# Border sums of residual times output: GpSimd products added by VectorE, or diagonals of TensorE products

## The reference, cut to what matters

```python
h = x
for layer in range(DEPTH):
    ...
    u = rms_norm_2(h, norm_g[layer, 0]) * (1.0 + sc1) + sh1
    ...
    y = mixer(u, ...)                       # ends with ... @ w_out
    h = h + (1.0 + g1) * rms_norm_2(y, norm_g[layer, 1])
    u = rms_norm_2(h, norm_g[layer, 2]) * (1.0 + sc2) + sh2
    y = swiglu_ffn(u, ffn_w_in[layer], ffn_w_out[layer])
    h = h + (1.0 + g2) * rms_norm_2(y, norm_g[layer, 3])
```

## Time and profile before

| | |
|---|---|
| median of 3 runs | 3499.42 us (3499.22 to 3500.74) |
| profiled execution | 3502.82 us, of it span 3501.0 us |
| mean granted TensorE clock | 0.973 |
| busy: PE, DVE, ACT, POOL | 95%, 57%, 37%, 2% of the span |
| POOL | 57.5 us in 59 instructions |

### The profile page before, as it was taken

How to read it: one execution, slowest core, us unless ns; L and a number is a source line. 1 busy time by engine, 2 the same in 40 slices (tenths; PEclk the granted TensorE clock), 3 DMA queues, 4 the chain that set the end, 5 groups by cost and what they waited for, 6 DMA issues and landing times.

```text
span 3501.0 us, 42504 instructions
## 1 busy us (share of the span) xinstructions
PE 3308.8 (95%) x17578; PEld 2729.0 (78%) x17578; DVE 2005.5 (57%) x2799; ACT 1312.5 (37%) x1947; POOL 57.5 (2%) x59
## 2 busy tenths in 40 slices
PE   7898988999999998999989999999899999889998
PEld 3685567888888755888887888888788888788887
DVE  6777665777556476565556656333654554563334
ACT  3323544231333245533355445222523332362223
POOL 0000000000000000000000010000100000010000
PEclk8999999999999999999999999999999999999999
DMA  4541022444444230265532222222143233223321
GB/s 175 178 139 43 13 79 67 157 151 155 148 157 138 82 88 3 95 209 186 174 90 69 73 73 85 97 96 88 53 103 86 68 91 78 64 75 106 97 94 52
DMA packets 374831, 356.11 MB, mean 102 GB/s; under 512 B 73407, under 2 KB 320494, under 8 KB 373231
## 3 DMA queue, kind: packets, MB, share of 16 engines
q1 hardware_dynamic: 374419, 353.32, 33.0%
q10 hardware_dynamic: 220, 0.07, 0.0%
HBM read 345.50 MB, written 4.72 MB: 100 GB/s over the span
## 4 chain that ended last, share of the span: by engine, by line
PE 49%; DVE 5%; ACT 4%; issue 1%; POOL 0%; DMA 0%; SPq 0%; ACTq 0%; DVEq 0%; POOLq 0%
PE ps L403 44%; PE ps L2715 1%; DVE r_st L2598 1%; PE ps L2736 1%; DVE second_w_lo L570 1%; ACT second_w_hi L511 1%; PE ps L2725 1%; ACT second_scr L712 1%; DVE sums L487 1%; DVE x_res L896 0%; PE ps L2738 0%; DVE second_scr L894 0%; POOL sq L470 0%; DMA ring<-in_ffn_w_in 0%; PE ps L2444 0%
## 5 line engine op out<-in xcount | busy, mean ns | idle before, releaser
L403 PE MATMUL ps<-second_h_hi,second_w_hi 128*128 128x512 f32 (+1 forms) x2216 | 823.9, 372 | 43.7 <-DVE second_h_lo L922 17.6
L403 PE MATMUL ps<-second_h_hi,second_w_lo 128*128 128x512 f32 (+1 forms) x2216 | 809.7, 365 | 0.0
L403 PE MATMUL ps<-second_h_lo,second_w_hi 128*128 128x512 f32 (+1 forms) x2216 | 809.4, 365 | 0.0
L570 DVE TENSOR_TENSOR second_w_lo<-ring,second_w_hi 128x2048 fp32r<-128x2048 f32 (+2 forms) x176 | 373.7, 2124 | 458.5 <-ACT second_w_hi L511 458.5
L403 PEld LDWEIGHTS ps<-second_h_hi,second_w_hi 128*128 128x128 f32 x2216 | 428.4, 193 | 109.7 <-issue 28.0
L403 PEld LDWEIGHTS ps<-second_h_hi,second_w_lo 128*128 128x128 f32 x2216 | 427.7, 193 | 65.7
L403 PEld LDWEIGHTS ps<-second_h_lo,second_w_hi 128*128 128x128 f32 x2216 | 428.5, 193 | 61.5
L511 ACT ACTIVATE second_w_hi<-ring 128x2048 fp32r<-128x2048 f32 (+2 forms) x176 | 311.9, 1772 | 289.3 <-PE ps L403 280.6
L403 PE MATMUL ps<-h_mix_hi,w_hi 128*128 128x512 f32 (+3 forms) x776 | 273.4, 352 | 20.5 <-DVE h_mix_lo L739 12.6
L403 PE MATMUL ps<-h_mix_lo,w_hi 128*128 128x512 f32 (+3 forms) x776 | 270.1, 348 | 0.0
L403 PE MATMUL ps<-h_mix_hi,w_lo 128*128 128x512 f32 (+3 forms) x776 | 269.3, 347 | 0.0
(11 more groups left out here) (451 smaller groups left out, 5402.1 us busy)
## 6 DMA issues: line engine op xcount, KB each, us to landing
ring<-in_w_mlp SPq DMA_DIRECT2D x64, 1024.0 KB, 5.3
side_w<-in_ada_w SPq DMA_DIRECT2D x96, 512.0 KB, 4.8
ring<-in_ffn_w_in SPq DMA_DIRECT2D x44, 1024.0 KB, 5.1
side_w<-in_w_mod SPq DMA_DIRECT2D x80, 512.0 KB, 3.8
ring<-in_attn_w_in SPq DMA_DIRECT2D x48, 512.0 KB, 5.2
ring<-in_hgrn_w_in SPq DMA_DIRECT2D x32, 512.0 KB, 4.9
ring<-in_ffn_w_out SPq DMA_DIRECT2D x16, 1024.0 KB, 4.9
ring<-in_w_in SPq DMA_DIRECT2D x14, 1024.0 KB, 5.5
```

Source lines behind the costliest of these rows:

```text
L403: mm = pe.matmul(acc, lhsT, rhs, start=k == 0 and wp == ap, stop=k == j.kt - 1 and wp == 1)
L570: dve.tensor_tensor(unit.place(unit.slot[1]), unit.place(M.ring[:, u % RING, :]), unit.place(unit.slot[0]), ALU.subtract).then_inc(*S.w_lo ...
```

## The change

POOL's products, and the middle part of DVE's adds, are gone. In their place PE multiplies, for each tile and half, x (128 features x 128 tokens, transposed) by g·y (128 x 128), in float32, and accumulates over the eight tiles in PSUM bank 6: the diagonal of each 128x128 result is the cross sum of these tokens, spread over partitions. DVE multiplies the two accumulated results of a half by the identity (`keep_cross`, one instruction of 128x256 out of PSUM), and PE's product with ones sums it (L845). A cross block stands in PE's list 0.8 of a job behind its tile and waits for ACT's g·y. The product with ones for Σ(g·y)² (L843) now follows half a position behind that for Σy² (L837) and waits for ACT's reading of the bank. DVE adds two parts instead of three and waits for ACT alone.

Two other tables change with it. FFN_PARTS is 3, 4, 4 units, so that a late job has 8 k steps, 24 products. LeaveThread starts half 0 4.5 positions behind its border, takes the first four feature tiles of both token groups first, so that it needs one residual batch to start, has ACT copy three blocks of four, and writes 512 features per DMA.

```diff
     def add_half(self, dve, j):
         S, acc = self.S, j.sums[3]
-        parts = slice(0, 1 if j.sums_last else 3)
...
+        parts = slice(0, 1) if j.sums_last else slice(0, 3, 2)
+        dve.wait_ge(S["sums_act"].sem, S["sums_act"].at(j.sum_nth + 1))
...
-    def add_sums(self, pool, j):
-        S = self.S
-        y, x, _, acc, fresh = j.sums
-        for sig, n in j.sums_after:
-            pool.wait_ge(sig.sem, sig.at(n))
-        pool.wait_ge(S["sums_act"].sem, S["sums_act"].at(j.sum_nth + 1))
-        if fresh:
-            pool.tensor_tensor(acc[:, 1, :], y, x, ALU.mult).then_inc(*S["sums_added"].one)
-            return
-        if not j.sums_last:
-            pool.tensor_tensor(self.scratch(j)[:, 1, :], y, x, ALU.mult).then_inc(*S["sums_product"].one)
...
         pe.matmul(M.ps[:, self.SUM_BANK, 0:b - a], M.ones[:, :], M.sums[:, 0, a:b], start=True, stop=True)\
             .then_inc(*S["norm_sum"].one)
         if self.last:
             return
-        for i in (1, 2):
-            mm = pe.matmul(M.ps[:, self.SECOND_BANK, (i - 1) * (b - a):i * (b - a)], M.ones[:, :], M.sums[:, i, a:b],
-                           start=True, stop=True)
-        mm.then_inc(*S["post_sum"].one)
+        yield self.start + 1.75
+        pe.wait_ge(S["norm_ln"].sem, S["norm_ln"].at(self.first + 1))
+        pe.matmul(M.ps[:, self.SUM_BANK, b - a:2 * (b - a)], M.ones[:, :], M.sums[:, 2, a:b], start=True, stop=True)
+        pe.wait_ge(S["cross_kept"].sem, S["cross_kept"].at(n + 1))
+        pe.matmul(M.ps[:, self.SUM_BANK, 0:b - a], M.ones[:, :], M.sums[:, 1, a:b], start=True, stop=True)\
+            .then_inc(*S["post_sum"].one)
+
+    def cross_products(self, pe):
+        S, M, n, a, b = self.S, self.M, self.post, self.a, self.b
+        for i, j in enumerate(self.tiles):
+            yield j.at + 0.8
...
+            pe.wait_ge(S["sums_act"].sem, S["sums_act"].at(j.sum_nth + 1))
+            k = j.where[0]
+            for c in range(a, b, P):
+                mm = pe.matmul(M.ps[:, self.CROSS_BANK, c:c + P], M.x[:, k, c:c + P], M.y[:, k, c:c + P],
+                               start=i == 0 and c == 0, stop=i == len(self.tiles) - 1, skip_group_check=True)
+        mm.then_inc(*S["cross_sum"].one)
+
+    def keep_cross(self, dve):
+        S, M, n, a, b = self.S, self.M, self.post, self.a, self.b
+        dve.wait_ge(S["cross_sum"].sem, S["cross_sum"].at(n + 1))
+        diagonal = M.ident[:, :].unsqueeze(1).to_broadcast([P, (b - a) // P, P])
+        dve.tensor_tensor(M.sums[:, 1, a:b].rearrange("p (i c) -> p i c", c=P),
+                          M.ps[:, self.CROSS_BANK, a:b].rearrange("p (i c) -> p i c", c=P), diagonal, ALU.mult)\
+            .then_inc(*S["cross_kept"].one)
...
-        self.items = [(2 * half + t, kh) for t in range(2) for kh in range(2)]
+        self.items = [(2 * half + t, kh) for kh in range(2) for t in range(2)]
...
-            if i == 0:
-                pe.wait_ge(S["post_x"].sem, S["post_x"].at(2 * self.border.post + 2))
+            if i in (0, 2):
+                pe.wait_ge(S["post_x"].sem, S["post_x"].at(2 * self.border.post + 1 + i // 2))
...
-FFN_PARTS = ((0, 4), (4, 4), (8, 3))
+FFN_PARTS = ((0, 3), (3, 4), (7, 4))
...
-        LeaveThread(R, B, dst, thread, half, thread.start + 3)
+        LeaveThread(R, B, dst, thread, half, thread.start + (4.5 if half == 0 else 3))
```

More of the change, by code:

```diff
@@ L592, in vector @@
             halves = [j] if self.added_by_dve(j) else []
-            if halves and not (j.at + 1 < len(self.jobs) and self.jobs[j.at + 1].sums):
+            if halves and (j.closes or not (j.at + 1 < len(self.jobs) and self.jobs[j.at + 1].sums)):
                 self.add_half(dve, j)
@@ L827, with __init__ @@
 class BorderThread(NormThread):
-    SECOND_BANK = 6
-    def __init__(self, R, y, last, *args):
-        self.y, self.last, self.sums = y, last, R.n_sums
+    CROSS_BANK = 6
+    def __init__(self, R, tiles, y, last, *args):
+        self.tiles, self.y, self.last, self.sums = tiles, y, last, R.n_sums
         self.post = R.posts
@@ L843, in tensor @@
         S, M, n, a, b = self.S, self.M, self.post, self.a, self.b
+        if not self.last:
+            yield from self.cross_products(pe)
         yield self.start + 1.3
@@ L876, in mean @@
         t, total, root = M.rs[:, LX:T], M.total[:, a:b], M.rs[:, a:b]
-        cross, square = (M.ps[:, self.SECOND_BANK, i * w:(i + 1) * w] for i in range(2))
+        cross, square = (M.ps[:, self.SUM_BANK, i * w:(i + 1) * w] for i in range(2))
         dve.wait_ge(S["post_sum"].sem, S["post_sum"].at(n + 1))
@@ L904, in vector @@
         S, n = self.S, self.post
+        if not self.last:
+            yield self.at(0)
+            self.keep_cross(dve)
         yield self.at(1)
@@ L937, in __init__ @@
         R.sides.append(self)
-    def engine(self, i):
-        return "act" if i % 2 else "dve"
     def kept(self, eng, n):
-        for name, count in (("left_by_dve", (n + 1) // 2), ("left_by_act", n // 2)):
+        by_dve = n // 4 + (n % 4 == 3)
+        for name, count in (("left_by_dve", by_dve), ("left_by_act", n - by_dve)):
             if count:
@@ L968, in scalar @@
     def scalar(self, act):
-        for i in (1, 3):
-            yield self.start + i // 2
+        for i in (0, 1, 3):
+            yield math.ceil(self.start) + i // 2
             to, src = self.keep(act, i)
@@ L974, in vector @@
     def vector(self, dve):
[L975 to L978, removed]
+        yield math.ceil(self.start) + 1
+        to, src = self.keep(dve, 2)
+        dve.tensor_copy(to, src).then_inc(*self.S["left_by_dve"].one)
     def sync(self, sp):
         S = self.S
[L982 to L986, removed]
+        for i, (t, kh) in enumerate(self.items):
+            yield self.start + 0.5 * i + 1
+            self.kept(sp, self.n0 + i + 1)
+            c = slice(kh * 512, (kh + 1) * 512)
+            sp.dma_start(self.dst[t][:, c], self.tok[:, t, c]).then_inc(*S.out.one)
         if self.half:
-            sp.wait_ge(S.out.sem, S.out.at(4))
+            sp.wait_ge(S.out.sem, S.out.at(8))
 class SplitThread(Thread):
@@ L2946, in summed @@
             j.sums = (M.y[:, b, a:e], M.x[:, b, a:e], M.gain2[:, gain, b:b + 1], M.sums[:, :, a:e], b == 0)
-            j.sums_last, j.slow = gain == 7, a > 0
+            j.sums_last, j.slow, j.gain_row = gain == 7, a > 0, gain
             j.sums_after = [(S["entered"], 2)] if gain == 1 else [(S["post_x"], gain - 1)]
@@ L2962, in border @@
     def border(half, at, scale=None, bias=None, limit=2 * N_LATE):
-        return BorderThread(R, lambda ks, a, b: M.y[:, ks, a:b], scale is None, lambda ks, a, b: M.x[:, ks, a:b], *half, D,
+        R.jobs[at].closes = True
+        tiles = [j for j in R.jobs if j.sums and j.gain_row == R.jobs[at].gain_row and j.where[1][0] <= half[0] < j.where[1][1]]
+        return BorderThread(R, tiles, lambda ks, a, b: M.y[:, ks, a:b], scale is None, lambda ks, a, b: M.x[:, ks, a:b], *half, D,
                             scale and (lambda k, a: M.gain2[:, scale, k:k + 1]), bias, scale and h, at, 0, limit, 0, 0)
```

27 lines of the change are left out of this document (16 added, 11 removed).

## The result

The changed kernel takes 3523.26 us in the median of 4 runs (3520.04 to 3524.51), the kernel before, on the same chip, 3500.08. One of the four runs of the kernel before was a slow one (11539.22 us), and the ratio on record is over the others: 1.0059 with a 95% interval of 1.0047 to 1.0071, slower by 0.6%, 16 to 25 us.

The account below looks back on a forecast made before the run. PE, busy 95% of the span, bounds the kernel, so gains come only where it stands still. Output 0 +5.25, output 1 +2.5, ffn 0 +2.1 and ffn 1 −1.6 sum to +8.2, 3507.6 us; range 3494 to 3515.

Parts of the forecast that it names:

- The walk through ACT's list: At the borders: ACT writes g·y late, so PE waits at cross blocks, 1.7, 0.8 and 2.45 us in output 0's half 1.
- The price of a product: On PE at every border: 0.223 us per float32 128x128 product, 96 products, 21.4 us in all.
- the waits of ffn 1 for copies: In ffn 1, half 0's blocks share a bank and wait for copies by ACT (1.9) and DVE (2.5): +4.4 us.
- The credit for the low clock: Slow stretches behind removed waits go: 1.6 us off output 0, 1.6 off ffn 0, and ffn 1's within its −5.0.
- Output 1: Output 1 with its border: half of output 0's cost, +2.5 us, since a block can hide in attention's last-input wait.
- rival A: Output 0, output 1 and ffn 0: most late g·y are not waited for; half the waits give 3495.6 us; chance 0.24.
- output 0: Output 0 with its border: +6.0 us up to the first sum, −0.75 from half 0's sum to half 1's, +5.25 together.
- ffn 0: ffn 0 with its border: 32 products, 7.1 us, and new waits, less 13.8 idle and 1.6 low clock: +2.1 us.
- The gain of the two other edits: ffn 1 and the end, with more products ahead of the transposes and leaving on one residual batch: −1.6 us.
- B: Whole kernel: PE loses all 34.8 us of old waits and never waits for g·y, −15 us, 3484; chance 0.12.
- C: Output starts and ffn 0: low clock behind new waits adds 5 to 6 us, 3513; chance 0.14 together with D.
- D: Whole kernel: POOL is off the path, PE pays 21.4 us and wins nothing, 3521; chance 0.14 together with C.

Follow-up runs that it names:

- e3: Changed kernel with each cross block two jobs later, whole computation kept: 3503.14 us, ratio 1.0004 to the kernel before.
- e11: e3 with only the products of a border's last tile, 84 of 96 left out: 3492.68 us, ratio 0.9972 to the kernel before.
- e1: Changed kernel multiplying x by x in the cross blocks, without the wait for ACT's g·y: 3501.49 us, ratio 0.9997 to the kernel before.
- e2: Changed kernel without all cross blocks but the last of each half: 3496.4 us, ratio 0.9987 to the kernel before.
- e7: Kernel before with the new FFN_PARTS and new LeaveThread, POOL's products kept, no cross blocks: 3494.59 us, ratio 0.998 to the kernel before.
- e9: e3 with the blocks of half 1's narrow tiles put back as in the changed kernel: 3507.16 us, ratio 1.0018 to the kernel before.
- e10: e3 with all blocks but those of half 1's narrow tiles put back as in the changed kernel: 3516.75 us, ratio 1.0047 to the kernel before.

## Why the prediction was wrong

The direction was right, with a chance of 0.48 for slower; the size was not: +8.2 forecast, about +20 measured, above the range's end.

**What held.** The walk through ACT's list. It gave new waits for g·y of 4.4 at output 0's start and 4.95 in its half 1; the profile has 0.18 + 1.87 + 1.88 and 1.87 + 0.58 + 2.51 (the second of these is in the trace between the two rows shown):

```profile
2119.16 0.35 PE L863 MATMUL ps<-second_y,x_res 128*128 128x128 f32 x1 [1.87 <-ACT second_y L451]
...
2129.33 0.35 PE L863 MATMUL ps<-second_y,x_res 128*128 128x128 f32 x1 [2.51 <-ACT second_y L451]
```

In ffn 0 it gave 8.85 and there are 1.29 + 0.44 + 3.98 + 2.20 = 7.9. The price of a product held (0.223 forecast, 0.22 by the rest of e3 against e11), and the waits of ffn 1 for copies: 1.9 and 2.5 forecast, 1.84 and 2.42 measured (L978 for `tok_out` in the list above). The credit for the low clock held in sum: three times 1.6, 4.8, were taken off, and 5 to 6 came back.

**Which steps failed.** Three stages were put too low; together they make up the miss of 11.4 us (19.6 − 8.2), with 1.3 of scatter and 1.5 that the end did better.

First and largest, "Output 1: I take half of output 0's, +2.5". It isn't half, it is nearly the same, +7.4. The reason given was that a block can hide in the wait for attention's last input. That wait, 1.83 before and 1.84 after, stands ahead of the wide tiles' last products, so no block that stands behind them hides in it. Behind them the kernel before has waits of 2.66 and 0.72 (us 3067 to 3076) for ACT's reading of the bank; the blocks' waits took their place. Before, and then after:

```profile
3067.86 0.39 PE L403 MATMUL ps<-second_h_hi,second_w_hi 128*128 128x256 f32 x1 [2.66 <-ACT sums L452]
```

```profile
3082.17 0.35 PE L863 MATMUL ps<-second_y,x_res 128*128 128x128 f32 x1 [2.05 <-ACT second_y L451]
...
3085.53 0.58 PE L863 MATMUL ps<-second_y,x_res 128*128 128x128 f32 x1 [1.87 <-ACT second_y L451]
```

So the idle time found there was used up by the new waits, not by the products, and their 32 times 0.22 us came on top. That is 4.9 of the 11.4 us. The prediction was at odds with itself here: its rival A counts the waits of output 1 "about as much again" as those of output 0, and its sum takes half. (Half of A's 29.4 us of waits is 14.7, too, not 12.)

Second, output 0, +9.05 for +5.25. Up to half 0's sum it is +7.2 for +6.0: the sum had put nothing for a low clock behind the new waits, and the stretch at 2090 cost 1.5 (the waits were 0.5 shorter than walked). Between the sums it is +0.8 for −0.75: the sum counts five blocks where six stand, and the stops cost more than their idle time. Behind half 1's sum it is +1.0, where the sum has nothing: PE waits there 0.42 at L843 and 1.61 for the next input's low half, where the kernel before had no wait.

```profile
2156.73 0.39 PE L404 MATMUL ps<-second_h_hi,second_w_hi 128*128 128x256 f32 x1 [1.61 <-DVE second_h_lo L943]
```

This wait is also in e1, e2, e3 and e11, and not at this place in e7, so it comes with the new border and not with the place of the blocks. DVE's chain to the next input (L899, before L881) starts 3.3 us after half 1's sum, right behind the last of the split products (L845), where it started 2.1 after it; and the slow stretch at 2130, by which PE had come to this point later, is gone.

Third, ffn 0, +4.9 for +2.1. Its idle time (−3.4 for −3.85) and its work (+7.9 for 7.6) came as forecast; the 1.6 of low clock taken off did not come (+0.5). As the low clock fell by more in output 1 than forecast, this moves a term between stages and doesn't explain the total.

One term erred the other way. The gain of the two other edits was under-estimated: −1.6 forecast (with 0.5 against it), −7 measured (e7). The walk was made in the changed kernel, where ffn 1 alone shows −3.1, and did not ask what the larger late jobs hide of ffn 0's 6.92 when no block stands in them.

**The rivals.** A (half of the waits don't come) fell: 28.4 us of them came (17.7 + 7.9 + 2.8), of 29.4 walked. B (faster) fell: even e3, which doesn't wait at its blocks, is at +1.4. C holds for single places, as at 2090 and 3084, but not as something on top of the sum, as other slow stretches went. D (PE pays 21.4 and wins nothing) comes within 2.3 us of the measured time and describes the net of the table: PE's work grew by 25.4 and its idle time fell by 1.3. Its reason, that POOL was off the path, is not what the runs show: e1 and e3 pay for the same 96 products, 13.8 and 11.2 us more of PE's busy time than before, and lose nothing.

**The sum by the runs.** Parts and leaving −7 (e7); POOL off and smaller adds −3 (e11 against e7, with 12 products in it); the other 84 products +11 (e3 against e11); their place +19, of it 14 to 15 at the starts and 4 to 5 in half 1 (e3, e9, e10). Together +20, the ratio's 20.6; each term carries an interval of some 3 to 6 us. What stays open is why the profiled executions put 9.8 on the starts in one comparison and 14.9 in the other.

## What to carry to other kernels

An instruction moved to the bounding engine can be paid twice, for its time and for its place: in a list that runs in order, put it behind the point where its operand is written, counted on the engine that writes it (here two jobs later, 19 us), not behind the point where the operand's source is ready. A wait is cheap where other waits follow that give way, and dear where the engine was running full. Read idle time, low clock and the rest of the engine's busy time apart for each stage: here idle time hardly changed, and the mean clock of the whole execution (0.973 and 0.974) hid that the stages lost 5 to 6 us less to the low clock. And run the side edits of a change by themselves: here they were the gain, and the title of the change was the loss.

## What was not expected of the hardware

After two waits of 2.05 and 1.87 us with one block and three products between them, PE was granted 0.50 over the 4 us from 3084 and 0.68 over the next 4 in output 1, while a single wait of 1.73 us in the kernel before was followed by products at full speed.
